# High and low weight parts of a chunk, made in two halves of 512 columns instead of whole

## The reference

```
proj = h @ w_in[l]
mix = jnp.concatenate([out_a, out_b, out_c], axis=-1) @ w_out[l]
x = x + rms_norm(memory_attention(h, m, w_mq[l], w_mk[l], w_mv[l], w_mo[l]), mem_norm_post[l])
a = h @ w_up                       # conv_ffn: 1024 -> 2 x 2816
return (jax.nn.gelu(gate) * val) @ w_down
proj = u @ w_in                    # short convolution: 1024 -> 4 x 2048
return (jax.nn.silu(z) * b_gate * y) @ w_out
proj = u @ w_in                    # mLSTM: 1024 -> 8200
```

## Time and profile before

| | |
|---|---|
| time, median of 3 runs | 951.14 us (950.74 to 952.48) |
| profiled execution | 951.14 us, of which 949.4 us from first to last instruction |
| granted TensorE clock, mean | 0.999 of full speed |
| TensorE busy | 931.6 us, 98% |
| VectorE busy | 658.7 us, 69% |
| ScalarE busy | 530.7 us, 56% |
| DMA queues | 166 GB/s, 48% of the engines' time |

### The profile page before, as it was taken

The page is one execution under the profiler, slowest core; times in us unless marked ns, Lnnn a source line. Parts: engine busy times, 40 slices in busy tenths (PEclk is TensorE's granted clock), DMA queues, the critical chain, the costliest instruction groups (busy, mean ns, idle before and its releaser), DMA issues.

```text
span 949.4 us, 19204 instructions
## 1 busy us (share of the span) xinstructions
PE 931.6 (98%) x7012; PEld 865.8 (91%) x7012; DVE 658.7 (69%) x1125; ACT 530.7 (56%) x892; POOL 118.4 (12%) x111
## 2 busy tenths in 40 slices
PE   7999999999999999999999999999999999999997
PEld 7988889997999998889999999999999998888885
DVE  5789867545799887447877777765667475776643
ACT  6767576545776665535444444444563566666552
POOL 2100010000165554000111111101010000000000
PEclk9999999999999999999999999999999999999999
DMA  8743334535255555552555555555455344445551
GB/s 315 248 163 133 118 109 146 163 115 186 84 201 195 194 180 199 198 199 90 185 171 177 173 177 174 173 183 178 137 197 186 126 172 140 149 140 160 175 196 46
DMA packets 44931, 157.91 MB, mean 166 GB/s; under 512 B 6051, under 2 KB 7075, under 8 KB 44620
## 3 DMA queue, kind: packets, MB, share of 16 engines
q1 hardware_dynamic: 44380, 155.56, 48.4%
q0 software_dynamic: 496, 1.59, 0.5%
HBM read 156.06 MB, written 1.06 MB: 166 GB/s over the span
## 4 chain that ended last, share of the span: by engine, by line
PE 92%; DVE 3%; ACT 3%; issue 1%; DMA 1%; SPq 0%; ACTq 0%; DVEq 0%
PE acc L1208 13%; PE acc L1209 12%; PE acc L1210 12%; PE scores L1208 5%; PE scores L1209 5%; PE scores L1210 5%; PE acc L1163 4%; PE acc L1161 4%; PE acc L1162 4%; PE scores L1163 2%; PE scores L1161 2%; PE scores L1162 2%; PE outs L1163 2%; PE outs L1162 2%; PE outs L1161 2%
## 5 line engine op out<-in xcount | busy, mean ns | idle before, releaser
L1735 DVE TENSOR_TENSOR w_lo<-raw,w_hi 128x1024 fp32r<-128x1024 f32 x288 | 352.9, 1231 | 104.2 <-ACT w_hi L592 103.7
L592 ACT ACTIVATE w_hi<-raw 128x1024 fp32r<-128x1024 f32 x288 | 302.3, 1055 | 158.4 <-PE acc L1210 71.2
L1208 PE MATMUL acc<-XH,w_hi 128*128 128x256 f32 (+1 forms) x632 | 181.3, 287 | 1.7 <-DVE w_lo L1735 1.0
L1209 PE MATMUL acc<-XL,w_hi 128*128 128x256 f32 (+1 forms) x632 | 179.6, 284 | 0.0
L1210 PE MATMUL acc<-XH,w_lo 128*128 128x256 f32 (+1 forms) x632 | 179.0, 283 | 0.0
L1208 PEld LDWEIGHTS acc<-XH,w_hi 128*128 128x128 f32 x632 | 119.1, 188 | 4.8 <-issue 2.3
L1208 PE MATMUL scores<-XH,w_hi 128*128 128x272 f32 (+1 forms) x424 | 120.8, 285 | 1.6 <-DVE w_lo L1735 1.6
L1209 PE MATMUL scores<-XL,w_hi 128*128 128x272 f32 (+1 forms) x424 | 120.8, 285 | 0.0
L1210 PE MATMUL scores<-XH,w_lo 128*128 128x272 f32 (+1 forms) x424 | 120.3, 284 | 0.0
L1209 PEld LDWEIGHTS acc<-XL,w_hi 128*128 128x128 f32 x632 | 119.0, 188 | 0.1
L1210 PEld LDWEIGHTS acc<-XH,w_lo 128*128 128x128 f32 x632 | 118.7, 188 | 0.0
(11 more groups left out here) (515 smaller groups left out, 1771.3 us busy)
## 6 DMA issues: line engine op xcount, KB each, us to landing
raw<-weights SPq DMA_DIRECT2D x288, 512.0 KB, 3.3
cst<-params SPq DMA_DIRECT2D x1, 1195.0 KB, 6.1
XR<-x_t SPq DMA_DIRECT2D x2, 512.0 KB, 6.2
Y<-mem_t SPq DMA_DIRECT2D x1, 1024.0 KB, 9.7
AR<-bias_rows POOLq DMA_DIRECT2D x4, 256.0 KB, 5.1
out<-AR SPq DMA_DIRECT2D x2, 512.0 KB, 3.0
AR<-final_gain POOLq DMA_DIRECT2D x1, 512.0 KB, 6.6
AR<-onehot SPq DMA_DIRECT2D x1, 66.0 KB
```

Source lines behind the costliest of these rows:

```text
L592: nc.scalar.activation(w_hi[:, n % SLOTS, :], raw[:, n % SLOTS, :], ACT.Copy).then_inc(hi_ready, 1)
L1208: nc.tensor.matmul(o, wh, h, start=start, stop=False)
L1209: nc.tensor.matmul(o, wh, l, start=False, stop=False)
L1735: V.tensor_tensor(w_lo[:, s, :], raw[:, s, :], w_hi[:, s, :].bitcast(F32), ALU.subtract).then_inc(lo_ready, 1)
```

## The change

`hi` issues two copies of 512 columns instead of one of 1024, and each counts `hi_ready` up, so that it now counts halves. `lo` issues two subtractions of 512 columns, each behind its own wait for the half of `w_hi` that it reads; the second alone counts `lo_ready` up, so that this still counts chunks. Nothing else changes: `chunk_done`, the loads and TensorE's instructions and waits are as before.

```
-                nc.scalar.activation(w_hi[:, n % SLOTS, :], raw[:, n % SLOTS, :], ACT.Copy).then_inc(hi_ready, 1)
+                for half in range(2):
+                    cols = span(half, 512)
+                    nc.scalar.activation(w_hi[:, n % SLOTS, cols], raw[:, n % SLOTS, cols], ACT.Copy).then_inc(hi_ready, 1)
...
             def lo(n, i=0):
 
-                dve.wait_ge(hi_ready, n + 1 + 4 * i)
                 s = n % SLOTS
-                V.tensor_tensor(w_lo[:, s, :], raw[:, s, :], w_hi[:, s, :].bitcast(F32), ALU.subtract).then_inc(lo_ready, 1)
+                for half in range(2):
+                    cols = span(half, 512)
+                    dve.wait_ge(hi_ready, 2 * n + half + 1 + 8 * i)
+                    last = V.tensor_tensor(w_lo[:, s, cols], raw[:, s, cols], w_hi[:, s, cols].bitcast(F32), ALU.subtract)
+                last.then_inc(lo_ready, 1)
```

## The result

| | before | after |
|---|---|---|
| median of 4 runs | 951.04 us (950.74 to 952.48) | 964.26 us (964.17 to 964.45) |
| ratio, 95% interval | | 1.0136 (1.0119 to 1.0154) |
| span of the profiled execution | 949.4 us | 962.6 us |
| granted TensorE clock | 0.999 | 0.998 |

The change makes the kernel 13 us slower. Forecast were 950.8 us and a range of 949.5 to 953.0, so the prediction is wrong in sign and in size.

A forecast was written before the change was run, and what follows sets the result against it. TensorE was taken to bound the kernel, losing 3.0 us to late w_lo. The places summed to -0.35 us, so span 949.05; with 1.7 us around it, 950.8 us, range 949.5 to 953.0.

The forecast's parts named there:

- The price of the split: VectorE, every chunk: two overlapping 512-column subtractions take 1.28 us against 1.22 whole, so 0.06 us per chunk, 17 us of VectorE's time.
- upper bound of 0.15: Split cost per chunk on VectorE if the two halves don't overlap at all: 2 x 0.683 - 1.22 = 0.15 us.
- (a): Start, TensorE at 13.13 after 1.02 us of idling: the pure w_hi to w_lo chain gets 0.37 us shorter.
- (b): TensorE's wait at 41.13: -0.37 us by itself, TensorE 0.19 us earlier after ScalarE's split costs; overwrites the start's gain, total -0.2.
- (c): TensorE's three waits for attention scaling L2112: work ahead of each 0.06 or 0.09 us longer, +0.24 us for the three.
- (d): 259.28, first chunks of the up stage, where VectorE has a queue of its own: +0.06 us, to +0.15.
- (e): First rounds of conv_in: TensorE starts 0.5 us before 455.33; the next w_lo leaves it 0.45 us earlier.
- Number 1: VectorE becomes the up stage's bound, from +0.16 us per split; with +0.30 the first 13 chunks lose, about 953.8 us; chance 0.11.
- Rivals 2: No overlap of halves, +0.15 us at each w_lo, but TensorE stays the bound: 951.4 us; chance 0.12.
- 3: Every late w_lo heals, winning 2.5 of TensorE's 3.0 us of waits for w_lo: 948.6 us; chance 0.06.
- 4: Nothing happens, as TensorE waits for whole chunks and the gain lies in idle time: 951.1 us; chance 0.14.

## Why the prediction was wrong

**What bounds the kernel.** Right: TensorE, and only late w_lo matter. It missed that the elementwise work of the up stage runs on three engines, of which two get in each other's way. GpSimd's row was read on the page and entered no sum.

**The price of the split, 0.06 us on VectorE.** This is the step that failed. It holds where GpSimd is idle or short: 1.28 us in the conv_in stage of the changed kernel, 1.29 in the run with short GpSimd operations. At the 41 pairs of the up stage that meet L557 or L559 it was 1.84 - 1.22 = 0.62 us, ten times as much and four times the upper bound of 0.15. That bound was made of rows in which nothing else disturbed VectorE (the earlier trace rows are at 814 us, where GpSimd has no work) and carried over to a stage with 22 us of GpSimd in 40. The register step and the second wait, on which the bound's doubt was put, cost nothing (the run with VectorE alone in halves lacks both and pays the same).

There was a sign in the trace of before, two lines below the w_lo of 292.19 in the earlier trace rows: L2209 took 0.63 us instead of the usual 0.47 when GpSimd (292.41, 1.60 us) was still at work.

```profile
293.66 0.63 DVE L2209 SCALAR_TENSOR_TENSOR AR<-AR,cst 128x255 f32<-128x255 f32 x1
```

GpSimd told the same of itself, in the first L557 of all, at a moment without a w_lo (VectorE's lines first):

```profile
256.45 0.42 DVE L2196 TENSOR_TENSOR AR<-scores,rstd 128x256 f32<-128x256 f32 x1
256.79 0.78 DVE L2209 SCALAR_TENSOR_TENSOR AR<-AR,cst 128x255 f32<-128x255 f32 x1
...
256.55 0.73 POOL L557 TENSOR_TENSOR AR<-AR 128x256 f32<-128x256 f32 x1 [108.81 <-ACT AR L912]
```

0.73 us here, 1.44 at 303.34. One and the same operation with twice the duration waits for somebody inside it. The lines also show for whom it doesn't: L2196, which reads one of its inputs from PSUM, is in hand when L557 asks, and neither is longer for it; L2209 behind it, with both inputs in SBUF, takes 0.78 us instead of 0.47. With halves these 0.16 us of L2209 go away (0.47 in the rows of after), which is why the period grows by 0.47 (2.64 to 3.11) and not by the full 0.62.

**The Trainium skill.** Its page SBUF — State Buffer, section "Who interferes with whom", says that a VectorE instruction with two inputs in SBUF and a GpSimd instruction that reads SBUF contend, through ports that are an exclusive lock; its section "SBUF: two separate sides" has it that whichever of the two starts first holds them for its whole instruction. The traces agree in every row above: GpSimd ends 0.60 or 0.61 us after the w_lo, or the part of one, that it found in hand, whatever that one's length; with the 272 columns of L569 it is 0.62 to 0.65. The prediction weighed two sections of the VectorE page and not this one, which speaks against the change. That it is the second input in SBUF that makes w_lo contend was not tried on w_lo itself; L2196 and L2209 above fit it. The runs show the exclusion, not the port. Of the Trainium skill's section "The DRAIN you can't avoid" (VectorE: DVE Perf Modes) the prediction took only the general sentence. The same section of the Trainium skill goes on to say that a next operation which isn't held starts earlier, and the 1.28 us for two of 683 ns agree with that.

**Place by place.** (a) 1.02 to 0.66, forecast 0.65; but TensorE starts at 13.15 against 13.13, because the first chunk of all, `kc0`, already starts 0.37 us later (9.19 against 8.81, waiting for XL). Why XL is later was not followed; the start at this place lies between 12.52 and 13.37 us in the experiments. The forecast of the gap holds, its effect on the time doesn't show. (b) 0.39 to 0.07; TensorE went on 0.30 us earlier, where 0.19 was forecast. (c) +0.24 forecast, the three waits grew from 1.2 to 1.5, right; but TensorE went from 0.30 us early at 49 us to 0.29 late at 216 us, 0.59 in all, so the stage lost more than these waits hold, and the rest wasn't followed. (d) +0.06 to +0.15 forecast, the wait went from 0.77 to 1.39, +0.62: the failed price in its first place, as that w_lo meets GpSimd's L559. (e) The first link, 0.78 to 0.35, is as forecast, 0.47 earlier; the next w_lo, said to be taken "as soon as it is there" and so to keep the gain, meets L569 and gives 0.59 back.

**The rivals.** Number 1, VectorE as the bound of the up stage, was the case. Its mechanism, its point of decision (0.16 us per split) and its stage were right, but its price was not: I gave it 0.30 us per split and 13 chunks, taking it that VectorE's idle time of 0.22 us later in the stage would carry it after that. VectorE's row of work without anybody's disturbance is 1.14 us from w_lo to the next operation (258.00 to 259.14 in the kernel before) and 1.35 from there to the next w_lo (303.36 to 304.71 above), 2.49 in all. That is 0.31 under TensorE's 2.80, and 0.62 more is 0.31 over it, at nearly every chunk; near the stage's end VectorE takes 3.00 per chunk (351.33 to 354.34), 0.2 over, to the last. Its sentence in favour, "POOL shares the stage", had no number. Rivals 2, 3 and 4 have fallen: the overlap of neighbours is real, the late w_lo don't all heal, and the waits do change.

**What would show it.** The test "wrong if w_lo's pairs take 1.38 us or more, or VectorE shows no idle time in the up loop's second half" named the two rows that did show it.

## What to carry to other kernels

Before an instruction is cut in two, look for whom its length keeps out: where another engine waits for its end, each seam is a door, and what comes through stands in the path of the second piece. A price read where the neighbour engines sleep holds only there; read it in the busiest stage, and put a number to each engine that works beside. And an operation that takes longer in one stage than its like in another tells, in the trace of before, that something is shared.

## What the hardware showed that was not expected

- GpSimd's 256-column operation takes 0.94 us or 1.47 us in the same place, with 0.6 us behind VectorE's end in both. The rest is waiting for VectorE, which the trace shows as busy time of GpSimd. A fall of GpSimd's busy time by 33 us (118.4 to 85.8) was the mark of a loss of 13 us.
- The order of arrival decides to within hundredths of a microsecond: 0.16 us into a pair with its seam at 0.20 us, GpSimd gets in and the pair takes 1.85 to 1.88; at 0.20 us it doesn't, and the pair takes 1.28.
- The number of columns ahead of the seam doesn't matter for VectorE: 128 + 896 and 512 + 512 take 1.28 us undisturbed, 512 + 512 and 768 + 256 take 1.84 disturbed.
- TensorE at 98% busy, as before, while it made 10% fewer products in a window: a wait of 0.26 us between chunks showed as 0.10, so busy time tells little and the count tells it. The busy time of its weight loads fell too, from 40.00 to 37.00 us in that window.
